# Softmax division ahead of the transpose, next pair's copies moved to the end of the pair, and a new order of the side engines' work in four attention stages

## The reference

```python
def softmax_attend(q, k, v, bias, mask, scale, sink=None):          # A, C, D
    s = einsum('...qgrd,...kgd->...grqk', q, k) * scale + bias
    s = where(mask, s, NEG_INF)
    p = softmax(s, axis=-1)        # D: one more column, the sink, dropped after the softmax
    return einsum('...grqk,...kgd->...qgrd', p, v)

def stick_breaking(q, k, v, q_pos, k_pos):                          # B
    z = einsum('bqhd,bkhd->bhqk', q, k) * q.shape[-1] ** -0.5
    log_beta, log_keep = log_sigmoid(z), log_sigmoid(-z)            # where visible
    w = exp(log_beta + (cumsum(log_keep, reverse=True) - log_keep))
    return einsum('bhqk,bkhd->bqhd', w, v)

for layer in (0, 1):
    x += concat(two attention groups of rms_norm(x)) @ w_out
    x += conv_ffn(rms_norm(x))     # up 1024 -> 5632, conv of width 3, SwiGLU, down 2816 -> 1024
y = rms_norm(x)
```

## Time and profile before

| | us |
|---|---|
| three runs, median (lowest, highest) | 3321.75 (3313.51, 3333.32) |
| profiled execution, its own time | 3322.09 |
| span of its trace | 3320.5 |
| PE busy | 3052.3 (92%) |
| DVE busy | 1766.5 (53%) |
| ACT busy | 953.4 (29%) |
| POOL busy | 630.9 (19%) |
| mean granted clock of PE | 0.969 |

### The profile page before, as it was taken

The page is one execution under the profiler, slowest core; times in us unless marked ns, Lnnn a source line. Parts: engine busy times, 40 slices in busy tenths (PEclk is TensorE's granted clock), DMA queues, the critical chain, the costliest instruction groups (busy, mean ns, idle before and its releaser), DMA issues. The chain is left out here.

```text
span 3320.5 us, 49778 instructions
## 1 busy us (share of the span) xinstructions
PE 3052.3 (92%) x17728; PEld 2597.0 (78%) x17728; DVE 1766.5 (53%) x3274; ACT 953.4 (29%) x2161; POOL 630.9 (19%) x352
## 2 busy tenths in 40 slices
PE   5888888889899999999999979988989999999997
PEld 4777777765699999999966545555569999999996
DVE  4333367774575555556541444545547655556555
ACT  3333367763321111111110124345432111111111
POOL 2111111100232332322300000000023222323320
PEclk8999999999999999999999999989999999999998
DMA  2111111000111111111011100000011111111111
GB/s 91 36 40 39 39 48 36 29 27 26 39 58 46 46 41 44 46 45 46 26 44 38 33 17 8 6 4 20 28 42 52 45 46 39 45 45 44 43 35 54
DMA packets 52790, 127.50 MB, mean 38 GB/s; under 512 B 11760, under 2 KB 19968, under 8 KB 52640
## 3 DMA queue, kind: packets, MB, share of 16 engines
q1 hardware_dynamic: 44160, 108.33, 10.2%
q0 software_dynamic: 5312, 16.80, 1.5%
q10 hardware_dynamic: 3168, 0.18, 0.1%
HBM read 111.52 MB, written 13.76 MB: 38 GB/s over the span
## 5 line engine op out<-in xcount | busy, mean ns | idle before, releaser
L1450 PE MATMUL ps<-hh,wh 128*128 128x384 f32 (+1 forms) x2112 | 697.5, 330 | 30.8 <-POOL wl L1571 17.7
L1450 PE MATMUL ps<-hl,wh 128*128 128x384 f32 (+1 forms) x2112 | 696.1, 330 | 0.0
L1450 PE MATMUL ps<-hh,wl 128*128 128x384 f32 (+1 forms) x2112 | 695.5, 329 | 0.0
L1571 POOL TENSOR_TENSOR wl<-raw,wh 128x1024 fp32r<-128x1024 f32 x132 | 382.4, 2897 | 1014.0 <-ACT wh L1505 1014.0
L1450 PEld LDWEIGHTS ps<-hh,wh 128*128 128x128 f32 x2112 | 400.0, 189 | 35.9 <-POOL wl L1571 18.8
L1450 PEld LDWEIGHTS ps<-hh,wl 128*128 128x128 f32 x2112 | 400.2, 190 | 0.0
L1450 PEld LDWEIGHTS ps<-hl,wh 128*128 128x128 f32 x2112 | 398.7, 189 | 0.4
L1505 ACT ACTIVATE wh<-raw 128x1024 fp32r<-128x1024 f32 x132 | 138.6, 1050 | 428.3 <-PE pot L1471 295.8
L295 PE MATMUL pot<-hh_mix,wh_mix 128*128 128x384 f32 (+1 forms) x576 | 210.3, 365 | 41.8 <-ACT q_next L332 15.9
L1515 ACT ACTIVATE tail<-u 128x2 f32<-128x2 f32 x88 | 17.9, 203 | 713.3 <-DVE u L1625 713.3
L1643 DVE SCALAR_TENSOR_TENSOR gates<-u,par,gates 128x1090 f32<-128x1090 f32 x88 | 203.9, 2317 | 3.1
(11 more groups left out here) (270 smaller groups left out, 5781.8 us busy)
## 6 DMA issues: line engine op xcount, KB each, us to landing
raw<-in_ffn_w SPq DMA_DIRECT2D x132, 512.0 KB, 3.2
w<-in_w SPq DMA_DIRECT2D x64, 256.0 KB, 2.6
w<-in_w SPq DMA_DIRECT2D x12, 512.0 KB, 3.6
w<-in_w_out SPq DMA_DIRECT2D x16, 256.0 KB, 2.7
strip<-in_bias POOLq DMA_DIRECT2D x5, 640.0 KB, 4.1
x<-in_x SPq DMA_DIRECT2D x4, 768.0 KB, 9.1
out_y<-x SPq DMA_DIRECT2D x2, 1536.0 KB, 6.3
out_bv<-vt POOLq DMA_DIRECT2D x4, 512.0 KB, 3.0
```

The source lines that it names most:

```text
L1450: mm = e.matmul(bank[:, 0:b - a], w[:, n % 3, k * P:(k + 1) * P], x[:, k, a:b], start=k == 0 and first, stop=k == KT - 1 and w is m.wl)
L1571: e.tensor_tensor(m.wl[:, n % 3, :], m.raw[:, n % 3, :], m.wh[:, n % 3, :].bitcast(F32), ALU.subtract).then_inc(self.low, 1)
```

## The change

It has five parts, all in the attention groups.

1. **Division ahead of the transpose** (A, C, D). `ve_scale` takes the reciprocal of the unit's row sum and multiplies the unit's whole weight tile by it in SBUF, in place; `pe_turn` waits for it (`scaled`) and no longer for the exponential. The diagonal, the matmuls with ones, the spread copy and DVE's multiplication go. `sc_output` is now one ACT copy from `po` to `o` in every group.
2. **Order of A, C and D.** On ACT the exponential stands ahead of `leave_next`. On DVE `ve_scale` and `ve_front` stand ahead of `leave_next` and of the output projection's `leave`.
3. **Early copies.** `move_scalar` and `move_vector` of pair j+1 move from the start of pair j+1 to the last steps of pair j, once its scores are done; q waits only for q's results, k only for k's.
4. **B one step on.** The copies of the transposed weights are done one step later on ACT and DVE, and so is PE's `pe_out`; the copy of an item waits for the `pe_out` of the tile before.
5. The first pair's copies stand ahead of the first `open`.

```diff
@@ Stream
     def move_scalar(self, e, p):
-        self.wait_left(e, p, len(self.results))
+        self.wait_left(e, p, 3)
     def move_vector(self, e, p):
-        self.wait_left(e, p, len(self.results))
+        self.wait_left(e, p, 9 if self.latent else 6)
+        if not self.latent:
+            e.wait_ge(m.cache_in, p * 32 + 32)
@@ Attend.pe_turn
-        e.wait_ge(self.probs, j * UNITS + u + 1)
+        e.wait_ge(self.scaled, j * UNITS + u + 1)
@@ Attend.pe_out
-        if self.kind != "B":
-            e.wait_ge(self.diagonal, j * NQT + t + 1)
-            m.apart(e)
-            for h in range(2):
-                e.matmul(m.po[HEAD * h:HEAD * h + HEAD, P:P + nq], m.ones[0:nq, 0:HEAD], m.diag[0:nq, h, 0:nq],
-                         start=True, stop=True, skip_group_check=True)
@@ Attend.scalar
-            st.move_scalar(e, j + self.p0)
...
         for step in range(-1, UNITS + 2):
+            if kind != "B":
+                self.sc_weights(e, j, step + 1)
             self.leave_next(e, "s", j, step, more)
...
+            if more and step == UNITS:
+                e.wait_ge(self.scores, j * UNITS + UNITS)
+                st.move_scalar(e, j + self.p0 + 1)
...
-                self.sc_weights(e, j, step + 1)
@@ Attend.vector
         for step in range(-1, UNITS + 2):
-            self.leave_next(e, "v", j, step, more)
-            if not more and self.tail and step <= UNITS:
-                self.tail.leave(e, j if kind == "D" else 0, step)
...
             elif kind == "C":
+                self.ve_scale(e, j, step)
                 self.ve_front(e, j, step + 1)
             else:
+                self.ve_scale(e, j, step)
                 if step == -1:
                     self.ve_front(e, j, 0)
                 self.ve_front(e, j, step + 2)
+            self.leave_next(e, "v", j, step, more)
+            if more and step == UNITS:
+                e.wait_ge(self.scores, j * UNITS + UNITS)
+                if kind == "A":
+                    e.wait_ge(self.kv_out, j * 64 + 64)
+                st.move_vector(e, j + self.p0 + 1)
+            if not more and self.tail and step <= UNITS:
+                self.tail.leave(e, j if kind == "D" else 0, step)
@@ ve_scale, in place of ve_diagonal and ve_keep
+        e.wait_ge(self.probs, j * UNITS + u + 1)
+        if kind == "D":
+            e.tensor_tensor(total, total, m.esink[0:nq, s8:s8 + 1], ALU.add).then_inc(self.inv, 1)
+            e.wait_ge(self.inv, j * per * UNITS + per * u + 1)
+        e.reciprocal(total, total).then_inc(self.inv, 1)
+        e.wait_ge(self.inv, j * per * UNITS + per * u + per)
+        e.tensor_scalar(wk, wk, total, None, ALU.mult).then_inc(self.scaled, 1)
@@ Sticks.tensor
-            if s - 3 in self.ends:
-                self.pe_out(e, j, self.ends[s - 3], more)
+            if s - 4 in self.ends:
+                self.pe_out(e, j, self.ends[s - 4], more)
@@ Sticks.read_item
+            if self.items[i][0]:
+                e.wait_ge(self.out, j * NQT + self.items[i][0])
@@ Sticks.scalar (and the same in vector, there at s == self.per + 1)
+            if more and s == self.per:
+                e.wait_ge(self.scores, j * self.per + self.per)
+                st.move_scalar(e, j + self.p0 + 1)
...
-            self.read_item(e, "s", j, s - 2, more)
+            self.read_item(e, "s", j, s - 3, more)
```

More of the change, by code:

```diff
@@ L429, in __init__ @@
         self.out, self.kept = sem("out"), sem("output_kept")
-        self.inv, self.diagonal, self.spread = sem("inverse"), sem("inverse_diagonal"), sem("inverse_spread")
+        self.inv, self.scaled = sem("inverse"), sem("scaled")
         self.qcopied = sem("q_copied")
@@ L689, in scalar @@
         self.open(e, j)
-        if st:
-            st.move_scalar(e, j + self.p0)
-        else:
+        if not st:
             e.activation(m.q[:, :], m.o[:, bass.ds(j + self.otile, 1), :], ACT.Copy).then_inc(self.qcopied, 1)
@@ L757, in sc_output @@
         e.wait_ge(self.out, j * NQT + t + 1)
[L758 to L762, removed]
+        m.apart(e)
+        e.activation(m.o[:, bass.ds(j + self.otile, 1), q0:q0 + nq], m.po[:, 0:nq], ACT.Copy).then_inc(self.kept, 1)
     def sc_weights(self, e, j, u):
@@ L833, in vector @@
         self.open(e, j)
[L834 to L837, removed]
         if kind == "A":
@@ L865, in vector @@
             if kind != "B":
[L866 to L869, removed]
                 self.read_unit(e, "v", j, step, more)
@@ L919, in ve_sticks, with ve_scale @@
         e.tensor_tensor(wk, self.m.ps[u % 2][0:nq, 0:w], wk, ALU.subtract).then_inc(self.mid, 1)
-    def ve_diagonal(self, e, j, t):
+    def ve_scale(self, e, j, u):
+        if not 0 <= u < UNITS:
+            return
         m, kind = self.m, self.kind
-        nq, s8 = self.nq(2 * t), (2 * t) % 8
-        total = m.rowsum[0:nq, s8:s8 + 2]
+        nq, w, s8 = self.nq(u), self.keys(u)[1] - self.keys(u)[0], u % 8
+        total = m.rowsum[0:nq, s8:s8 + 1]
+        wk = self.wk(u)[0:nq, 0:w]
         per = 2 if kind == "D" else 1
-        e.wait_ge(self.probs, j * UNITS + 2 * t + 2)
+        e.wait_ge(self.probs, j * UNITS + u + 1)
         if kind == "D":
-            e.tensor_tensor(total, total, m.esink[0:nq, s8:s8 + 2], ALU.add).then_inc(self.inv, 1)
-            e.wait_ge(self.inv, j * per * NQT + per * t + 1)
+            e.tensor_tensor(total, total, m.esink[0:nq, s8:s8 + 1], ALU.add).then_inc(self.inv, 1)
+            e.wait_ge(self.inv, j * per * UNITS + per * u + 1)
         e.reciprocal(total, total).then_inc(self.inv, 1)
[L932 to L947, removed]
+        e.wait_ge(self.inv, j * per * UNITS + per * u + per)
+        e.tensor_scalar(wk, wk, total, None, ALU.mult).then_inc(self.scaled, 1)
     def gpsimd(self, e, j, more):
@@ L1041, in tensor @@
         st.wait_moved(e, j + self.p0)
-        for s in range(-2, self.per + 3):
+        for s in range(-2, self.per + 4):
             if s % 2 == 0 and s + 2 < self.per:
@@ L1122, in scalar @@
         self.open(e, j)
-        st.move_scalar(e, j + self.p0)
         if more:
             st.wait_moved(e, j + self.p0)
-        for s in range(-2, self.per + 5):
+        for s in range(-2, self.per + 6):
             if more:
@@ L1135, in scalar @@
                 self.read_v(e, "s", j)
-            self.read_item(e, "s", j, s - 2, more)
-            if s - 4 in self.ends:
-                self.sc_output(e, j, self.ends[s - 4])
+            self.read_item(e, "s", j, s - 3, more)
+            if s - 5 in self.ends:
+                self.sc_output(e, j, self.ends[s - 5])
     def size(self, i):
@@ L1171, in vector @@
         self.open(e, j)
-        e.wait_ge(m.cache_in, (j + self.p0) * 32 + 32)
-        st.move_vector(e, j + self.p0)
         if more:
             st.wait_moved(e, j + self.p0)
-        for s in range(-2, self.per + 5):
+        for s in range(-2, self.per + 6):
             if more:
@@ L1181, in vector @@
                     self.tail.leave(e, 0, n + 1)
+            if more and s == self.per + 1:
+                e.wait_ge(self.scores, j * self.per + self.per)
+                e.wait_ge(self.kv_out, j * 64 + 64)
+                st.move_vector(e, j + self.p0 + 1)
             self.ve_sum(e, j, s)
@@ L1185, in vector @@
                 self.read_v(e, "v", j)
-            self.read_item(e, "v", j, s - 2, more)
+            self.read_item(e, "v", j, s - 3, more)
     def ve_cap(self, e, j, i):
@@ L1891, in _ @@
                     st.first(e, "s")
+                    st.move_scalar(e, 0)
                     a.pairs(e, a.scalar)
@@ L1911, in _ @@
                     st.first(e, "v")
+                    st.move_vector(e, 0)
                     a.pairs(e, a.vector)
```

## The result

The changed kernel takes 3356.95 us (median of four runs, 3348.51 to 3360.64), the kernel before beside it 3317.63 us. The ratio is 1.0106, 95% interval 1.0078 to 1.0134: slower by 1.1%, outside the predicted range. The profiled execution took 3360.64 us with a span of 3359.1 us, 38.6 us more than before's 3320.5.

A forecast was written before the change was run, and what follows sets the result against it. PE's own work plus its gaps was taken as the bound, no side engine. A -41, C +43, D +8, B -19 and clock +7 made -2: 3320 us, with a range of 3294 to 3348 leaving two in ten out.

The forecast's parts named there:

- A: Attention group of four pairs: waits for front and product, ones and q copy go, -10.0 us per pair, -41 us in all.
- C: Attention group where PE would wait for the late-emptied bank: +13.7 us per pair, three times +41, +43 us in all.
- D: Attention group with DVE's addition behind scale and front: +5.2 less 2.5 and 0.5, +2 per pair, +8 us.
- B: Attention group without the division: bank emptied sooner, waits for scores gone, shorter pair starts, -19 us.
- the clock term in C: New stops in C: half of nine bring a 3.4 us stretch at 1.2 GHz, +5 per pair, +15 us.
- The chain through front, exponential and copy: In C, PE stands until the side engine has emptied the bank: 2.85 us at 768 columns, 19.2 us per pair.
- rival 2: Each new stop in C and D brings the slow clock: +30 us or more over three pairs, 3345 us; chance 0.20.
- C's last pair: Five emptyings behind a front, about 1.7 us each, +8.5, less 2.5 and 1.5 of division waits: +4.5 us.
- the cover that I had taken for granted: Transposes of a unit come later than its scale; without it, up to 0.8 us each, 14 us per C pair.
- The bound of +60 for C: Upper bound of C's loss, if each of 9 waits cost the 3.4 us of the widest.
- the -8 for the clock: In A, five starts get B's 3.4 us slow stretch in place of 6.8, saving 1.7 us each.
- Held scales (rival 3): In A, 24 GpSimd splits each hold a scale by up to 1.1 us; half uncovered gives 3333 us; chance 0.06.

## Why the prediction was wrong

**The step that failed is the clock term in C**: "if half of the nine bring a stretch of 3.4 us, it is +5 per pair, +15". Two things were wrong in it. By its own numbers it is too small: half of nine stretches at 1.7 us each are 7.7 us a pair, 23 in all, which would have put the sum at 3328 us. And it priced the stretches too short. Among the 27 stops of the three pairs stand 14 stretches, about half as I had said, but seven of them are 6.8 us long and seven 3.4. I had priced all by B's 3.4, though A's 6.8 stood in the same rows. With those at the starts the three pairs ran 23.9, 34.1 and 34.1 us at 1.2 GHz against 6.8, 10.2 and 6.8 before. Half of the differences is 34 us where I had 15. Without this term the three pairs lost 73.6 - 34.1 = 39.5 us; my +13.7 per pair made 41. The chain through front, exponential and copy was right almost stop by stop (18.1 us against 19.2, the place of the earlier trace rows 2.78 us against 2.8, the widest 3.3 against 3.4), and so was the sign in C.

What happened is rival 2, with 0.20, at 3345 us; it priced the clock at 15 to 30 us a pair, and it was 11. Five stops of 2.1 us and more stood on my own list for each pair (2.1, 2.7, 2.7, 2.9, 3.4), and behind B's single stop of 2.1 us there was a slow stretch in my own rows, so it deserved more than 0.20. The Trainium skill, TensorE: Matmul & The Clock Gate, section "A second HAM failure mode: psum-queue depth-cycling", says that frequent short idle spells between groups of matmuls make the clock go down and up again. The trace agrees: no stop of the bank's nine is over 3.3 us, and five stretches at 1.2 GHz stand among them.

**C's last pair** I costed at +4.5 for five emptyings of the bank. There are none: the output projection has its matmuls in D. What the last pair did get is 2.4 us of transposes that wait for the scale, in five stops: the cover that I had taken for granted fails here as well. It became 2.5 us shorter all the same, with 3.4 us at 1.2 GHz instead of 17.1. The kernel with C's copies first has the same instructions in this pair, but 13.7 us at 1.2 GHz, and takes 57.7 us, only 0.3 less than before. So most of the 2.5 us is the clock. C's entry gained nothing, where I had -2. The bound of +60 for C was too low by its own terms, too: nine waits of 3.4 us, less what came off, make +75 in the three pairs. Together the errors in C are +12.4 us: three pairs 73.6 against 56.1, the last -2.5 against +4.5, the entry -0.1 against -2.

**D** +13.8 us instead of +8. The late addition cost what I had forecast: +5.2 us a pair, in five stops (6.1 us where there were 1.9; I had 7.1). What fell short is the division's side: with the addition put back first, a pair of D is 1.6 us shorter than before, and I had taken off 3.0. That is the 1.4 us a pair by which D is over.

**A** -41.3 us. The -41 was met, but the -8 for the clock didn't come on top. In the pair shown the front's 3.3 us went, `pe_out` kept 1.4 of 3.9 us (the earlier trace rows without the 0.8 for the copied weights have 3.1), the ones' 2.5 went, the start fell from 3.0 to 2.3 us instead of 1.9 and ends now in the meeting of the engines (`POOLq L520` is `open`'s drain on GpSimd) rather than in a copy, and a transpose waits 0.4 us longer: 8.6 us instead of 10. The clock gave about the rest: 30.6 us at 1.2 GHz in the four pairs where there were 41.0, worth 5 us, where I had 8 on top of the 41. What I had right only by luck is the cover of the scale: the division-only kernel shows that it rests on the order.

**B** -15.0 instead of -19. The waits for the bank didn't fall at all: 2.0 + 1.4 + 0.8 us in the pair shown, where the earlier trace rows have 3.6 and I took back 2.2. What B gained is 0.8 us at each start, 0.9 of the scores' 1.5, less slow clock (3.4 and 0 us in two pairs, 6.8 and 3.4 before), and in its last pairs the addition of the output projection, 1.9 us of waits instead of 4.3.

**Held scales (rival 3).** Not decisive. All scales of A's four pairs and their durations:

```profile
L930 DVE TENSOR_SCALAR wk<-wk,rowsum x72: 285/552/1135, 108.5 to 381.5; 128x640 f32<-128x640 f32 x32, 128x128 f32<-128x128 f32 x8, 128x256 f32<-128x256 f32 x8, 128x384 f32<-128x384 f32 x8
```

Eight were held: four of 256 columns took 1.13 us and the other four 0.35, four of 512 took 0.72 and the other four 0.49. All eight overlap one of GpSimd's splits (`wl_mix<-w,wh_mix`, L315), and none of the other 64 does. The diagonals before had eight as well, 1.39 us each. So it is one scale in nine, eight in all and not 24, and no transpose in A's four pairs waited for a scale.

**The sum.** Forecast against measured: C +12.4, D +5.8, A +7.7, B +4.0, feed-forward 0 +0.5 and +9.7 us behind D, in all 40.1 of the 40.6 between forecast and span. The +9.7 stands behind the groups that the change touches; whether the changed program brings its eight stops isn't shown. Without it the profiled time would be some 3351 us, still outside the range. The range ended at 3348 although the prediction's own bounds (+60 in C, +16 in D, +30 for the clock) reached far beyond.

## What to carry to other kernels

When one PSUM bank passes from PE to a side engine and back, the copy that frees it has to stand ahead of anything on that engine that waits for PE's newest work; what may stand ahead of it depends on how far ahead that work was handed over. One order helped in A (front a tile ahead, 10 us a pair gained with the division) and hurt in C (front of the scores just done, 22 to 26 us a pair lost). When a change brings several stops of 2 to 3 us a pair, cost the slow clock as well, and by every length that a slow stretch has in your rows: here 11 us a pair for 16 us of added stops. And change the order in one stage at a time: here the gains of A, B, the division and the early copies hid behind the new order in C and D, and with that put back the kernel is 1.9% faster than before.

## What the runs showed of the hardware

- Nine stops of 0.8 to 3.3 us in 102 us: five stretches at 1.2 GHz (27.3 us) stand among them, in which PE worked. Where 17 unread matmuls ran in seven of these stops there was none, and the pair was 11.4 us shorter with all else in place. The stretch at the start of a pair is there in both.
- The slow clock is not fixed by the program: two pairs with the same instructions and the same stops differ by 17.1 against 6.8 us of it, and by 5.3 us in length. C's last pair, the same in two kernels, had 3.4 us of it in one and 13.7 us in the other, with granted clocks of 0.96 and 0.87, and took 55.5 and 57.7 us.
- Scaling a float32 tile in SBUF in place on VectorE took 0.29, 0.35, 0.42, 0.49 and 0.55 us for 128, 256, 384, 512 and 640 columns. While GpSimd was at a split of a weight tile, it took 1.13 us for 256 and 0.72 for 512.
- A feed-forward block that no version touches took 833 to 835 us in three kernels and 839 to 843 in seven, with three or four short stops of PE in the one case and eight in the other. The cause is open.
